# Square sums left to TensorE, top-k rounds drawn forward, and the hidden stores issued by ScalarE

## The reference, cut to what matters

```python
# GLA: each head's output is normed over its 256 features, then gated by silu(r)
o = _rmsnorm(o, norm_g.reshape(GLA_HEADS, dvh)).reshape(B, S, GLA_DV)
ya = (o * jax.nn.silu(r)) @ w_branch_a
# sparse attention: the 128 keys of highest score, of those not later than the query
rel = relu(einsum('bqhd,bsd->bqhs', iq, ik) * IDX_DIM ** -0.5)
score = where(key_pos <= t, einsum('bqh,bqhs->bqs', iw * IDX_HEADS ** -0.5, rel), -inf)
_, idx = lax.top_k(score, min(DSA_TOPK, S // 4))
y = (sigmoid(za) * ya + sigmoid(zb) * yb) @ w_out
# experts
a = gelu(einsum('td,thkd->thk', h, u)) * gates
out = einsum('thk,thkd->td', a, v)
```

## Time and profile before

| | |
|---|---|
| median of 3 runs | 2128.53 us (2128.34 to 2128.91) |
| the profiled execution | 2128.34 us, of which the profile's span is 2126.6 us |
| TensorE busy | 2099.1 us, 99% of the span |
| VectorE, ScalarE, GpSimd busy | 1612.3 us, 970.8 us, 402.0 us |
| GLA stage, selection stage | about 300 to 485 us, 485 to 608 us |
| `U` stage, `V` stage | about 965 to 1590 us, then to the end |

### The profile page before, as it was taken

One profiled execution on the slowest core, in us unless ns is written; L12 is line 12 of the kernel. 1 busy time (PEld: TensorE's weight loads), 2 busy tenths in 40 slices (PEclk: granted clock), 3 DMA queues, 4 the chain that ended last, 5 costly groups with the idle time before them and its releaser, 6 DMA issues.

```text
span 2126.6 us, 29016 instructions
## 1 busy us (share of the span) xinstructions
PE 2099.1 (99%) x10931; PEld 1833.4 (86%) x10931; DVE 1612.3 (76%) x2965; ACT 970.8 (46%) x1701; POOL 402.0 (19%) x296
## 2 busy tenths in 40 slices
PE   8999999999999999999999999999999999999998
PEld 6877788887877788789999999999998888888886
DVE  4777576665985544799999988777668888888887
ACT  5444454544234423433366657766533433333333
POOL 2000110000000001000232323222223344444440
PEclk9999999999999999999999999999999999999999
DMA  6411144431331122123778988898999999999993
GB/s 257 157 49 43 50 163 179 172 125 60 109 109 41 45 95 99 63 97 117 260 283 278 328 286 301 293 313 289 348 366 373 366 371 372 376 376 378 376 361 145
DMA packets 137435, 471.50 MB, mean 222 GB/s; under 512 B 10112, under 2 KB 59520, under 8 KB 111568
## 3 DMA queue, kind: packets, MB, share of 16 engines
q1 hardware_dynamic: 50512, 309.39, 39.8%
q0 software_dynamic: 36864, 134.23, 16.3%
q10 hardware_dynamic: 49920, 26.01, 4.2%
HBM read 417.04 MB, written 52.43 MB: 221 GB/s over the span
## 4 chain that ended last, share of the span: by engine, by line
PE 91%; DVE 7%; ACT 1%; issue 1%; DMA 0%; SPq 0%; DVEq 0%; ACTq 0%
PE bank L156 89%; DVE whl L309 1%; PE bank L668 1%; DVE L L1480 1%; DVE L L1478 1%; DVE room L2121 1%; DVE room L2117 0%; PE bank L1569 0%; DMA XT<-in_xT 0%; DVE L L1461 0%; DVE row L2177 0%; DVE wk L1853 0%; DVE fg L2128 0%; DVE cidx L1851 0%; PE bank L2383 0%
## 5 line engine op out<-in xcount | busy, mean ns | idle before, releaser
L156 PE MATMUL bank<-xhl,whl 128*128 128x384 f32 (+1 forms) x5304 | 1089.0, 362 | 13.2 <-DVE whl L519 8.0
L156 PEld LDWEIGHTS bank<-xhl,whl 128*128 128x128 f32 x5304 | 946.4, 189 | 105.5 <-issue 9.4
L309 DVE TENSOR_TENSOR whl<-raw,whl 128x1024 fp32r<-128x1024 f32 (+2 forms) x389 | 468.7, 1214 | 218.3 <-ACT whl L302 179.4
L156 PE MATMUL bank<-whl,ag 128*128 128x512 f32 x2304 | 526.2, 390 | 1.0 <-issue 0.5
L156 PEld LDWEIGHTS bank<-whl,ag 128*128 128x128 f32 x2304 | 431.4, 188 | 91.5 <-ACT whl L302 2.2
L302 ACT ACTIVATE whl<-raw 128x1024 fp32r<-128x1024 f32 (+2 forms) x389 | 394.4, 1032 | 87.9 <-PE bank L156 79.8
L2164 POOL DMA_INDIRECT row<-in_U_rows,row_at x128 | 177.6, 1388 | 603.9 <-DVE row L2177 429.8
L2164 POOL DMA_INDIRECT row<-in_V_rows,row_at x128 | 183.1, 1431 | 259.1 <-DVE y_tok L2193 228.9
L2193 DVE SCALAR_TENSOR_TENSOR y_tok<-row,row_a,y_tok 128x1024 f32<-128x1024 f32 x127 | 162.4, 1279 | 2.7
L2177 DVE SCALAR_TENSOR_TENSOR row<-row,h_tok 128x1024 f32<-128x1024 f32 x128 | 155.7, 1217 | 0.1
L2239 ACT ACTIVATE h_both<-bank 128x384 f32<-128x384 f32 x128 | 62.7, 490 | 155.5 <-PE bank L156 151.6
(11 more groups left out here) (270 smaller groups left out, 1954.2 us busy)
## 6 DMA issues: line engine op xcount, KB each, us to landing
raw<-in_U SPq DMA_DIRECT2D x64, 1024.0 KB, 6.8
raw<-in_V SPq DMA_DIRECT2D x64, 1024.0 KB, 6.8
hidden<-h_both SPq DMA_DIRECT2D x32, 768.0 KB, 9.8
gates<-g_stage ACTq DMA_DIRECT2D x12, 2048.0 KB, 18.5
g_ring<-gates SPq DMA_DIRECT2D x32, 768.0 KB, 10.9
h_ring<-hidden SPq DMA_DIRECT2D x22, 768.0 KB, 8.3
raw<-in_w_ada SPq DMA_DIRECT2D x16, 1024.0 KB, 6.3
raw<-in_w_gla SPq DMA_DIRECT2D x12, 1024.0 KB, 4.9
```

What stands on the lines that cost most here:

```text
L156: return e.matmul(o, a, b, start=start, stop=stop, skip_group_check=True)
L309: e.tensor_tensor(lo[:, s], src[:, s], F(hi[:, s]), ALU.subtract).then_inc(dve_lo.of((i, half)))
```

## The change

Three edits that do not touch each other. The GLA square sums: VectorE's addition is gone, and TensorE sums both halves itself, with eight float32 products in place of four; it waits for ScalarE's squares. The selection: the rounds drawn per loop grow from (5, 6, 7, 5) to (6, 7, 8, 8) before the second split and from (3, 3, 3, 2) to (3, 3, 4, 4) behind each gate product; a draw when nothing is left does nothing. The hidden stores: the DMA is issued by ScalarE right behind the fourth `hide` of a group, on ScalarE's queue, after a wait for that `hide` to finish; SyncE's `store` is gone.

```diff
         def gla_sums(e, q, h):
-            b = gla_banks.fill(q, ("norm", h))
-            q.wait_ge(dve_gla["squares", h])
-            square_sums(e, q, b, 0, gla_sets[h % 2][5][:, 0:T], True).then_inc(pe_gla.of(("sum", h)))
+            b, vtok = gla_banks.fill(q, ("norm", h)), gla_sets[h % 2][5]
+            for half in range(2):
+                q.wait_ge(act_gla["square", h, half])
+                m = square_sums(e, q, b, 0, vtok[:, half * T:(half + 1) * T], half == 0)
+            m.then_inc(pe_gla.of(("sum", h)))
...
-                e.tensor_tensor(vtok[:, 0:T], vtok[:, 0:T], vtok[:, T:2 * T], ALU.add).then_inc(dve_gla.of(("squares", h)))
...
-                for _ in range((5, 6, 7, 5)[n]):
+                for _ in range((6, 7, 8, 8)[n]):
                     next(picks, None)
...
-                    for _ in range((3, 3, 3, 2)[n]):
+                    for _ in range((3, 3, 4, 4)[n]):
                         next(picks, None)
...
         def sync_u(e, q):
-            def store(g):
-                q.wait_ge(act_u["h", g, 3])
-                e.dma_start(hidden[g], h_stage[g % 2]).then_inc(put_hidden[g % 2].of(g), 16)
...
                 load_raw(e, q, 87 + 2 * g)
-                if g > 0:
-                    store(g - 1)
                 load_raw(e, q, 88 + 2 * g)
-            store(NG - 1)
             load_group(e, q, 2)
...
                 e.activation(h_stage[g % 2][:, n * TD:(n + 1) * TD], u_banks.of["h", g, n][:, 0:TD], ACT.Gelu
                              ).then_inc(act_u.of(("h", g, n)))
+                if n == 3:
+                    q.wait_ge(act_u["h", g, 3])
+                    e.dma_start(hidden[g], h_stage[g % 2]).then_inc(put_hidden[g % 2].of(g), 16)
```

## The result

The changed kernel takes 2142.93 us (median of 4 runs, 2141.73 to 2144.80) beside 2128.72 us for the kernel before: a ratio of 1.0067, 95% interval 1.0050 to 1.0085, or +14.2 us. I had forecast slower by 0.26%, 2134.1 us within 2129.0 to 2137.1. The direction is right and the size is not: the time lies above the range.

A forecast was written before the change was run, and what follows sets the result against it. The prediction took TensorE, busy 99% of the span, as the bound, so only its waits and added work count. Sums +1.0, rounds +4.1 and stores +0.5 gave +5.6 us: 2134.1 us median, range 2129.0 to 2137.1.

The forecast's parts named there:

- Part A: GLA square sums: head 2 gains 2.0 us, heads 0, 1 and 3 lose 3.0 us together; net +1.0 us.
- Part B: Selection: added rounds delay VectorE's splits, so TensorE's block for `w_ba` 3 starts late; +4.1 us, not absorbed later.
- the rival that is not slower: Selection's end: rounds behind the last gate product do hold the attention stage, so time returns; 2129.2 us, chance 0.06.
- The rival of a fall in selection: TensorE's clock falls at selection's new waits, 1.7 us per fall; with head 2's kept, 2135.5 to 2137.1 us; chance 0.15.
- Part C: Hidden stores: ScalarE's wait and issue, about 0.5 us per group, vanish except at one place; +0.5 us.
- The place that I had named for the 0.5, at 1021: A group's late fourth Gelu before a high half; through VectorE, TensorE's 0.9 us wait for `fg` grows by 0.5.
- The rival of the shared queue: Hidden stores queue behind gates stores on ScalarE's queue and land too late for buffer reuse; 2145 us, chance 0.05.
- lead of 9.4 us: While gates are spread, ScalarE's one-hot tile is scaled 9.4 us ahead of its matmul, so 0.5 us vanishes there.

The follow-up runs named there:

- E3: The kernel before with only the square sums changed (TensorE sums both halves, no VectorE addition): ratio 1.0001 (0.9992 to 1.0010).
- E12: The kernel before with fewer early rounds, (3, 4, 5, 3) in place of (5, 6, 7, 5) ahead of the second split: ratio 1.0015, +3.2 us.
- E10: The kernel before with one round less ahead of the first loop's second split, (4, 6, 7, 5): ratio 1.0000 (0.9991 to 1.0009).
- E1: The changed kernel with the hidden stores back on SyncE, new sums and rounds kept: ratio 1.0026 to the kernel before, +5.5 us.
- E4: The kernel before with only the rounds drawn earlier: ratio 1.0027 (1.0017 to 1.0038), +5.7 us.
- E2: The kernel before with only the hidden stores moved to ScalarE: ratio 1.0031 (1.0019 to 1.0043), +6.6 us.
- E5: The kernel before with 24 hidden stores issued by ScalarE; the eight held in the changed kernel stay on SyncE: ratio 1.0005 (0.9996 to 1.0014).
- E7: E2's kernel with each 2 MB gates store cut into two of 1 MB: ratio 1.0004 to the kernel before (0.9995 to 1.0014).
- E9: E2's kernel with each 2 MB gates store written in whole rows, output order altered: ratio 1.0002 to the kernel before (0.9992 to 1.0011).
- E6: The kernel before with only the eight hidden stores held in the changed kernel issued by ScalarE, 24 by SyncE: ratio 1.0046, +9.8 us.

## Why the prediction was wrong

**Part A, the sums: the mechanism held, the size was close.** Each of heads 0, 1 and 3 pays 1.71 - 0.82 = 0.89 us (1.0 forecast; the 0.82 is head 3's eight records before, 478.15 to 478.97). Head 2 gains 2.1 to 2.3 us (2.0 forecast). The net is +0.4 to 0.6 us (1.0 forecast), and E3 can't tell it from nothing. The clock stayed up behind sixteen narrow products.

**Part B, the rounds: right.** From the start of the block of `w_za` 1 to the next stage the kernel before needs 607.56 - 541.18 = 66.38 us, the changed one 612.28 - 541.75 = 70.53: +4.15 us against 4.1. The idle time at the end of the rounds was TensorE's pace, as I had read it, so the rival that is not slower fell. E12 shows that rounds left there do hold the next stage once there are eight more; between one more (E10, without a wait there) and eight nothing was tried.

**The clock.** The rival of a fall in selection fell: waits of 1.12 to 1.44 us among dense matmuls kept the upper level, in the changed kernel as in E1 and E4. In head 2, 1.27 us were enough in the kernel before and in the eight other traces that have that wait, and 2.53 us were enough in `U`. A wait's length alone doesn't decide.

**Part C, the stores: the step that failed.** I put "the issue of one DMA (0.37 us for the one on its queue now)" at about 0.5 us per group. The row was that of a gates store which found its queue empty. The issue behind a gates store is another case: eight times 1.0 to 9.2 us. In the trace it costs 1.1 + 4.3 us, in E2 +6.6 us (4.0 to 9.2), not 0.5. With it the sum would have been about 1.0 + 4.1 + 0.5 + 5.4 = 11.0 us, near the trace's 10.5. The place that I had named for the 0.5, at 1021, did what I wrote: the wait for `fg` grew from 0.9 to 1.4 us. It is 1.4 us too in E2, E5, E7 and E9, where ScalarE issues that group's store, and 0.9 in E1 and E6, where SyncE does.

The rival of the shared queue had the right pair of stores, and a price of 2145 us near the 2142.9 measured, but a chance of 0.05 and another mechanism: a buffer whose store lands too late, so that ScalarE waits for a landing before its next Gelu. No such wait is in the trace. ScalarE is held earlier, at the issue. I had also taken its lead of 9.4 us as cover. It is about right, and a hold of 9 us followed by a split and a scaling uses it up. At 1213.57 and 1254.01 holds of 8.74 and 8.76 us cost TensorE nothing: the next tile was scaled some 0.4 us ahead of its matmul. At the two places that cost, ScalarE had just waited 2.38 and 2.37 us for VectorE's tile (ahead of 1170.03 and of 1294.76), and the lead falls short.

The Trainium skill's rule which stood beside that rival (page "DMA: Bandwidth & Descriptors", section "Queues, rings and completion order": one row of rings per issuing engine, taken in order) fits the traces: while the two kinds of store stood on different queues, no issue of a hidden store took over 1.6 us (at most 1.59 in the kernel before, 1.23 in E1 and 1.22 among the 24 that SyncE issues in E6).

**What stays open.** The four timed runs are 2.8 to 5.9 us over the profiled execution, which the trace can't explain. Two readings stand side by side, neither of them shown. The holds differ by execution (8.93 us in the changed kernel, 10.20 in E2, 9.77 in E6 at the same store), and a longer hold can cost TensorE its whole length. And executions differ ahead of anything that the edits touch: TensorE starts its block of 48 projections at 315.68 us in the trace of before and at 315.85 in that of after, but at 319.68 in E1, 320.84 in E4 and 320.69 in E6, behind a stretch of narrow float32 products in which the clock is down for longer (granted clock 0.66 from 280 to 290 us in E1, 0.83 before). The two traces that the result compares are the two quickest there. How many pieces the queue takes before an issue is held wasn't measured.

## What to carry to other kernels

An engine that computes should not issue a DMA on a queue on which a transfer of many small pieces may still stand: here the issue held the engine for up to 10.26 us, with no semaphore to show for it. The length of the issuing instruction in the trace tells it, and larger pieces cured it (E9), as did another queue (E1). And where a second engine feeds TensorE just in time, each piece of its later work drawn ahead of a feed delays TensorE by its length, less what slack the feed had. The idle time at the end of that engine's work is where such a piece costs nothing, as long as it fits in: one round did, eight didn't.

## What the runs showed of the hardware

- The issue of a 768 KB store took 0.33 us on a free queue of ScalarE and up to 10.26 us (E6) behind a 2 MB store of 512-byte pieces on the same queue; with the same 2 MB in whole rows it took 0.33 us right behind it (E9). It was held every time that it came within 6.2 us of such a store, and 7 us behind one sometimes 1.0 to 4.3 us and sometimes not at all.
- TensorE's clock kept its upper level over waits of 1.41 us among 512-column matmuls and of 1.38 us among 384-column ones (E2). It fell to the lower one behind a wait of 1.27 us among narrow float32 products, in each of nine traces, and behind waits of 2.53 us in `U` and 2.68 us in the attention stage (E12).
